# Two transformer blocks on one core: latents' norms in halves, the bias store and the recurrence's weights moved, decay and bonus a round later, feed-forwards begun by channel blocks

## The chip, the core and the metric

The program runs on one core of a Trainium2 chip. A core has five engines that follow their own instruction streams and meet only at semaphores: TensorE (PE in the profile) multiplies matrices into PSUM banks, VectorE (DVE) and ScalarE (ACT) do elementwise work and reductions, GpSimd (POOL) does slower elementwise work, and SyncE (SP) issues DMA transfers. ACT and POOL issue DMAs too. The metric is the device time of the whole program in microseconds (us), and the number that is compared is the median over several executions.

## What is computed

x is 1024 tokens by 1024 channels, everything is float32, and two layers run one after the other. The reference, cut:

```python
# first block
mod = silu(c) @ ada_w + ada_b                 # 1024 -> 6144: six vectors
h = rms_norm(x, mix_pre_norm) * (1 + sc_m) + sh_m
att_p, rwkv_p = split(h @ w_in)               # 456 and 1824 columns
# attention: latents cq (256), ckv (128), index key (64), each with an rms norm
score = sum_h iw[h] * relu(iq[h] @ ik.T)      # causal; the top 256 keys of each query are kept
logits = qa @ ckv_sel + rel_bias[bucket(t - s)]
# recurrence (RWKV7, 8 heads of 64), on p + mu * (p_prev - p)
S = S * w_t + (S @ a_t) b_t + v_t k_t ;  y_t = S @ r_t
y = (groupnorm(y) + sum(r * k * r_k) * v) * g # the sum is the "bonus"
x = x + g_m * rms_norm(concat(att, y) @ w_out)
f = (silu(hf @ w_gate) * (hf @ w_up)) @ w_down    # hf = modulated rms_norm(x), 2816 hidden
x = x + g_f * rms_norm(f)
# second block: short convolution, attention by chunks, gated mix, then
up = causal_conv3(rms_norm(h) @ w_ffn_up) + b     # 2 x 2816
h = h + rms_norm((gelu(f_gate) * f_val) @ w_down) # and a gated per-layer embedding
```

## The kernel before

The kernel is written by hand in one order per engine. Each operation that another waits for raises a counter (`V.up(name)`, `S.up(name)`, `T.up(name)`), and `wait_ge(*X.at(name))` waits for it. An engine never goes past its waiting instruction. `B.free(b)` and `B.until(b, ...)` guard the eight PSUM banks.

**Projection and rows, 0 to 440 us.** x is normalized and transposed to hT. Weights come in pieces of up to 1 MB into five slots. `ROW_LOADS` is the order in which SP issues these loads (`ring_load`, L419), `SLOT_OF` says which slot a piece takes, and SP waits there until the piece that held the slot has been used. PE computes the attention columns (L523), then eight tiles of the first 256 recurrence columns (`("rkv", 0, t)`), then three small matmuls (L579) that turn the relative bias into a row for each head. ACT copies this row (L1021) and issues one DMA (L1023) that stores it 128 times into `bias_rows`, 4.6 MB in all, on its own queue. Attention reads `bias_rows` much later. Then come `LAT_STEPS`: transposes of the normed latents ("turn") and the index queries ("iq"), with one of the `ROW_STEPS` behind every second. Then the index scores with lora columns among them, then the lora columns 1 and 2, then the rest of `ROW_STEPS`. These 56 steps are 40 `("rkv", c, t)`, 256 columns of one token tile, and 16 `("mod", j, q)`, pieces of the modulation whose weights (`in_ada_w`) fill a slot each. An `rkv` step is a group of matmuls on L523, a `mod` step one on L483, with its sum (L502 or L508) behind it.

**The top 256 of each row** are found on DVE by `best_rows`, a generator. Each `next(K.best)` is a pass: count passes (L854, L858) of a bisection, with half of the counting on ACT (`K.sums`, L872), and at the end 24 rank passes (L925 to L937). 223 are needed. The numbers of passes are written out: 30 beside the loras, `passes_beside(i)` beside each row step i, `best_steps(g)` in each round of the recurrence.

**Recurrence, 440 to 866 us.** Eight token tiles go through rounds; tile t starts 7 rounds after tile t - 1. `front_*` (j = 0 to 6) makes the tile's rows, `free_*` the 64 x 64 products (L1266, L1352), `state_*` the state. The fronts of tile 0 lie beside the last row steps (`round_beside`), from i = 43 on. In `front_vector`, j = 4 ends with Pe (L1609), Pm (L1610), krow (L1613) and the bonus sum (L1615). `front_pool` at j = 0 mixes the keys (L1666, L1668), and at VALUES (6, for tile 0: 8) the values (L1673 to L1677).

**The feed-forwards** start at 1150 us (first block) and at 2753 us (second). The normed tokens of a tile (`("normed", ...)`) are transposed by PE (L2319), scaled by DVE (L2333) and ACT (L2347) into `turned`, split into a high and a low part (L2103 on ACT, L2110 on DVE) for a block k of 128 channels and half the tokens, and multiplied by three weight blocks (L2071, L2073, L2075).

Of the kernel before, what the change touches and what calls it, by code (L numbers as in the profile page):

```python
# [19 lines left out]
FILL = -3.0e38  # L20
# [188 lines left out]
def layout(nc, I, out):  # L209
# [52 lines left out]
    scr = region(W1 - 3440, W1)  # L262
# [15 lines left out]
    r = region(HI0, W1 - 3440)  # L278
# [11 lines left out]
    K.top = region(W1 - 48, W1).take("top", 8, 6)  # L290
    K.lprev, K.ikk = K.rl[0], K.rl[1].rearrange("p (t n) -> p t n", t=8)
# [147 lines left out]
def proj_sync(sp, K):  # L439
# [87 lines left out]
def proj_tensor(pe, K):  # L527
# [39 lines left out]
    w, landed = ring_tile(K, ("rkv", 0), 8, 256)  # L567
    pe.wait_ge(*landed.at(("rkv", 0)))
    for t in range(NT):
        b = 2 + (4 + t) % 6  # L570
        pe.wait_ge(*B.free(b))
        token_group(pe, K, b, w, 256, t).then_inc(*T.up(("rkv", 0, t)))
        B.until(b, S, ("rkv", 0, t))
    T.mark(("free", ("rkv", 0)))
    pe.wait_ge(*D["hot"].at("hot"))
    for i, o in enumerate(range(0, 1152, 512)):
        n = min(512, 1152 - o)
        pe.wait_ge(*B.free(2 + i))
        mm = pe.matmul(bank(K, 2 + i)[0:8, 0:n], K.relb[0:33, :], K.oh[0:33, o:o + n], start=True, stop=True, skip_group_check=True)  # L579
        B.until(2 + i, S, ("bias", i))  # L580
    mm.then_inc(*T.up("bias"))
    pe.wait_ge(*V.at("latents"))
    pe.wait_ge(*V.at("modulation 0"))
    for i, step in enumerate(LAT_STEPS):
        lat_tensor(pe, K, step, 2 + 2 * (i % 2))
        if i % 2:
            row_tensor(pe, K, ROW_STEPS[i // 2], ROW_BANK[i // 2])
# [124 lines left out]
def proj_vector(v, K):  # L712
# [51 lines left out]
    v.wait_ge(*S.at(("att", 1, 7)))  # L764
    sq = K.stage[0]
    for j, (a, n, dst) in enumerate(((0, 256, K.att[:, :, 0:256]), (256, 128, K.ckv), (384, 64, K.ikk[:, :, 0:64]))):
        x_ = K.att[:, :, a:a + n]
        v.wait_ge(*V.own())
        v.tensor_tensor(sq[:, :, 0:n], x_, x_, MUL).then_inc(*V.up())
        v.wait_ge(*V.own())  # L770
        v.tensor_reduce(K.st[:, 0:8], sq[:, :, 0:n], AX, ADD).then_inc(*V.up())
        v.wait_ge(*V.own())
        variance(v, K, ("lv", j), K.st[:, 0:8], n, 1e-6)
        v.wait_ge(*G.at(("lr", j)))
        v.tensor_tensor(dst, x_, b8(K.st[:, 16:24], n), MUL).then_inc(*V.up())
    v.wait_ge(*V.own())
    v.wait_ge(*D["m2"].at("m2"))
    v.tensor_tensor(K.ckv, K.ckv, K.kvB.unsqueeze(1).to_broadcast([128, 8, 128]), MUL).then_inc(*V.up())
    v.tensor_tensor(K.ikk[:, :, 0:64], K.ikk[:, :, 0:64], K.ikB.unsqueeze(1).to_broadcast([128, 8, 64]), MUL).then_inc(*V.up())
    v.wait_ge(*V.own())  # L780
    v.tensor_copy(K.ikk[:, :, 64:128], K.ikk[:, :, 0:64]).then_inc(*V.up())
    v.tensor_scalar(K.iw, K.att[:, :, 448:456], float(8 ** -0.5 * 64 ** -0.5), None, MUL).then_inc(*V.up("latents"))
    for i, step in enumerate(LAT_STEPS):
        lat_vector(v, K, step, 2 + 2 * (i % 2))
# [8 lines left out]
    for i in range(ROWS_FIRST, len(ROW_STEPS) + 1):  # L793
        if i == ROWS_FIRST + 4:
# [31 lines left out]
def passes_beside(i):  # L826
    return 4 if ROW_STEPS[i - 1][0] == "rkv" and i <= BESIDE else 2
# [2624 lines left out]
```

## Time and profile before

| | |
|---|---|
| median of 3 runs | 3649.11 us (3641.34 to 3659.92) |
| the profiled execution: its time, its span | 3646.83 us, 3645.5 us |
| PE busy, DVE busy, ACT busy | 3346.4, 1794.3, 928.1 us |
| chain of work that ended last | PE 81%, DVE 11%, ACT 4% |
| TensorE clock, mean over the span | 0.962 of full |

The profile shows one execution. The span is the time from the first to the last instruction. Its stages have different limits, so a stage is read by itself: the windows give busy time and clock of a stretch, the timeline shows behind each row in square brackets how long the engine sat idle before it and what ended that.

### The profile page before, as it was taken

How to read it: one execution, taken by the hardware profiler on the slowest of the kernel's cores; microseconds unless marked ns; L12 is line 12 of the kernel's file. 1: busy time of each engine (PE TensorE's matmuls, PEld its weight loads, DVE VectorE, ACT ScalarE, POOL GpSimd, SP SyncE). 2: the span in 40 equal slices, each digit the busy share in tenths (PEclk: the TensorE clock that was granted, in tenths of full speed). 3: DMA queues.
4: the chain of work that ended last, by engine and by line, in shares of the span. 5: the costliest groups of instructions: out<-in, count | busy, mean ns of one | idle time of the engine just before them, and what ended most of it. 6: DMA issues, size and time to landing. Idle time of an engine off the chain costs nothing.

```text
span 3645.5 us, 51038 instructions
## 1 busy us (share of the span) xinstructions
PE 3346.4 (92%) x21635; PEld 2602.0 (71%) x21650; DVE 1794.3 (49%) x2850; ACT 928.1 (25%) x1709; POOL 339.0 (9%) x278
## 2 busy tenths in 40 slices
PE   7988867887888999999999889999998999999998
PEld 6736655775567788888886556876676888878876
DVE  2378677664556322224545546321246444444656
ACT  2255432333534100001222544000025111111122
POOL 0000245762001000000000000000000000000000
PEclk9989977999999999999999999999999999999999
DMA  6337210101114111113331001111133111123434
GB/s 216 70 65 239 84 42 19 37 20 59 47 64 133 52 47 52 47 47 104 121 118 50 4 24 40 42 35 35 58 116 110 47 47 52 47 75 98 140 115 144
DMA packets 217381, 270.18 MB, mean 74 GB/s; under 512 B 11229, under 2 KB 176387, under 8 KB 216900
## 3 DMA queue, kind: packets, MB, share of 16 engines
q1 hardware_dynamic: 211851, 247.87, 21.3%
q10 hardware_dynamic: 3192, 11.17, 1.7%
q0 software_dynamic: 2112, 7.87, 0.6%
q8 instruction: 173, 2.83, 0.3%
q14 instruction: 53, 0.43, 0.0%
HBM read 232.80 MB, written 34.08 MB: 73 GB/s over the span
## 4 chain that ended last, share of the span: by engine, by line
PE 81%; DVE 11%; ACT 4%; issue 2%; DMA 1%; POOL 1%; SPq 0%; DVEq 0%; ACTq 0%; POOLq 0%
PE psum L2071 18%; PE psum L2073 18%; PE psum L2075 18%; PE psum L523 5%; PE psum L3089 3%; PE psum L1266 2%; PE psum L2589 2%; PE psum L2910 2%; PE psum L2797 2%; PE psum L651 1%; PE psum L1821 1%; PE psum L2926 1%; DVE Lg L1915 1%; PE psum L1847 1%; DMA slot<-in_ada_w 1%
## 5 line engine op out<-in xcount | busy, mean ns | idle before, releaser
L2071 PE MATMUL psum<-hT_hi,wcut_lo 128*128 128x512 f32 x1856 | 589.4, 395 | 16.7 <-DVE hT_lo L2110 16.7
L2073 PE MATMUL psum<-hT_hi,wcut_hi 128*128 128x512 f32 x1856 | 582.8, 391 | 0.0
L2075 PE MATMUL psum<-hT_lo,wcut_hi 128*128 128x512 f32 x1856 | 582.5, 391 | 0.0
L2071 PEld LDWEIGHTS psum<-hT_hi,wcut_lo 128*128 128x128 f32 x1856 | 350.4, 189 | 97.0 <-DVE hT_lo L2110 17.9
L2053 DVE CAST wcut_hi<-raw 128x1024 fp32r<-128x1024 f32 x256 | 176.9, 691 | 478.6 <-PE psum L2075 454.0
L2075 PEld LDWEIGHTS psum<-hT_lo,wcut_hi 128*128 128x128 f32 x1856 | 350.3, 189 | 73.2
L2073 PEld LDWEIGHTS psum<-hT_hi,wcut_hi 128*128 128x128 f32 x1856 | 350.3, 189 | 72.6
L2071 PE MATMUL psum<-wcut_hi,xcut_lo 128*128 128x512 f32 x1120 | 348.7, 393 | 17.6 <-DVE xcut_lo L2189 13.8
L2073 PE MATMUL psum<-wcut_hi,xcut_hi 128*128 128x512 f32 x1120 | 347.2, 392 | 0.0
L2075 PE MATMUL psum<-wcut_lo,xcut_hi 128*128 128x512 f32 x1120 | 346.9, 391 | 0.0
L1097 POOL TENSOR_TENSOR st<-st,nhalf 128x1 f32<-128x1 f32 (+2 forms) x78 | 61.1, 790 | 2827.2 <-DVE st L709 2827.2
L2055 DVE TENSOR_TENSOR wcut_lo<-raw,wcut_hi 128x1024 fp32r<-128x1024 f32 x256 | 313.8, 1226 | 8.8
L2071 PEld LDWEIGHTS psum<-wcut_hi,xcut_lo 128*128 128x128 f32 x1120 | 211.5, 189 | 63.4 <-DVE xcut_lo L2189 15.7
L2073 PEld LDWEIGHTS psum<-wcut_hi,xcut_hi 128*128 128x128 f32 x1120 | 211.9, 189 | 44.3
L2075 PEld LDWEIGHTS psum<-wcut_lo,xcut_hi 128*128 128x128 f32 x1120 | 211.6, 189 | 44.1
L523 PE MATMUL psum<-slot,hT 128*128 128x256 f32 (+1 forms) x1024 | 230.7, 386 | 3.3 <-DMA slot<-in_w_in 3.3
L523 PEld LDWEIGHTS psum<-slot,hT 128*128 128x128 f32 x1024 | 196.5, 197 | 37.7 <-issue 13.7
L2160 ACT ACTIVATE xcut_hi<-fS 128x512 fp32r<-128x512 f32 x88 | 55.1, 632 | 329.8 <-PE psum L2075 325.8
L2495 ACT ACTIVATE fS<-psum 128x1024 f32<-128x1024 f32 x22 | 22.7, 1030 | 427.9 <-PE psum L2075 427.9
L2486 DVE TENSOR_TENSOR fS<-fS,psum 128x1024 f32<-128x1024 f32 x22 | 26.9, 1221 | 190.9 <-PE psum L2075 190.9
L872 ACT ACTIVATE counted<-counted 128x1024 bf16<-128x1024 bf16 (+2 forms) x99 | 93.0, 941 | 70.0 <-DVE counted L854 69.8
L2521 DVE SCALAR_TENSOR_TENSOR tb<-psum,CF,tb 128x1023 f32<-128x1023 f32 x22 | 28.2, 1283 | 135.4 <-ACT tb L2541 135.4
(428 smaller groups left out, 4354.5 us busy)
## 6 DMA issues: line engine op xcount, KB each, us to landing
raw<-in_w_ffn_down SPq DMA_DIRECT2D x88, 512.0 KB, 3.6
raw<-in_w_ffn_up SPq DMA_DIRECT2D x66, 512.0 KB, 3.8
slot<-in_ada_w SPq DMA_DIRECT2D x24, 1024.0 KB, 11.7
raw<-in_w_in SPq DMA_DIRECT2D x28, 512.0 KB, 5.4
raw<-in_w_ffn_gate SPq DMA_DIRECT2D x22, 512.0 KB, 3.9
slot<-in_w_in SPq DMA_DIRECT2D x8, 1024.0 KB, 6.1
raw<-in_w_out SPq DMA_DIRECT2D x16, 512.0 KB, 3.7
x_one<-xrow SPq DMA_DIRECT2D x16, 512.0 KB, 2.8
```

The lines of the kernel that those rows point to most:

```text
L523: mm = pe.matmul(p[:, 0:n], K.hT[:, k, t * 128:(t + 1) * 128], w[:, k, 0:n], start=k == 0, stop=k == 7, skip_group_check=True)
L872: s.activation(a, a, ACT.Copy, accum_out=K.top[:, 0, t - 2:t - 1]).then_inc(*K.S.up(("counted", n, t)))
L1266: mm = pe.matmul(b0[par][half(c), cols64(q, o)], lhs(c, q, par), rhs(c, q, par), start=start, stop=stop, skip_group_check=True)
L2053: v.tensor_copy(hi, raw).then_inc(*K.V.up())
L2055: v.tensor_tensor(lo, raw, hi.bitcast(F), SUB).then_inc(*K.V.up(("cut", name, n)))
L2071: pe.matmul(outs[i], al, bs[i][0], start=start, stop=False, skip_group_check=True)
L2073: pe.matmul(outs[i], ah, bs[i][0], start=False, stop=False, skip_group_check=True)
L2075: mm = pe.matmul(outs[i], ah, bs[i][1], start=False, stop=stop, skip_group_check=True)
L2589: mm = pe.matmul(bank(K, t)[:, 0:n], K.hT2[:, k, t * 128:(t + 1) * 128], w[:, k, :], start=k == 0, stop=k == 7, skip_group_check=True)
L2797: mm = pe.matmul(bank(K, b)[:, 0:n], xT[:, k, t * 128:(t + 1) * 128], w[:, k, :], start=k == 0, stop=k == kt - 1, skip_group_check=True)
L2910: mm = pe.matmul(bank(K, b, 2)[:, o:o + n], K.qT[0:96, h, t * 128:(t + 1) * 128], K.kT2[0:96, h, o:o + n], start=True, stop=True, skip_gro ...
L3089: mm = pe.matmul(bank(K, b, 2)[:, h], K.wo[q % 2][j][:, k, :], xT[:, k, h], start=k == 0, stop=k == 3, skip_group_check=True)
```

## The change

Four things are changed.

1. The latents' norms are done in two halves of four tiles (`norms_vector`), beside the copies of the attention columns. The eight `("rkv", 0, t)` steps now lie among `LAT_STEPS`, and no row step does; all 56 row steps come behind the loras. The bias matmuls, their copies and the store of `bias_rows` lie between the loras and the first row step.
2. `rwkv_weights`, eleven loads on SP's queue that wait for ("shift", 2) on DVE, are issued behind the load of `("mod", 3, 2)`, ahead of that of `("mod", 3, 3)`. The store of the latents is moved ahead of them, the wait for the bias store behind them. The mod steps are spread over 24 rkv steps.
3. 180 passes instead of 140 beside the row steps, and two in each round of the recurrence instead of three (fourteen rounds) or two: 53 were left for it, now 13. krow and bonus go from front round 4 to 5. POOL mixes a tile's keys behind the values of the tile before, and tile 0's values one round earlier.
4. Both feed-forwards begin by channel blocks: PE transposes block k of four tiles into one bank, DVE scales it, ACT and DVE split it, and PE multiplies it by all three weight blocks. Before, weight block 0 came first with all k, then 1, then 2.

Core of the diff:

```diff
-LAT_STEPS = [("turn", t) for t in range(NT)] + [("iq", q) for q in range(4)]
+LAT_STEPS = [("rkv", 0, t) for t in range(5)] + [("turn", 0), ("turn", 1), ("rkv", 0, 5), ("turn", 2), ("turn", 3), ("rkv", 0, 6),
+             ("turn", 4), ("turn", 5), ("rkv", 0, 7), ("turn", 6), ("turn", 7)] + [("iq", q) for q in range(4)]
...
-        if (1, 5) <= (_c, _t) < (3, 5):
+        if _c < 4 and (8 * _c - 8 + _t) % 3:
             ROW_STEPS.append(_mods[sum(s[0] == "mod" for s in ROW_STEPS)])
...
-SLOT_OF = {_s: (1, 3, 4)[_i % 3] for _i, _s in enumerate(_mods)}
-SLOT_OF.update({("rkv", _c): 2 * (_c % 2) for _c in range(2, 6)})
+SLOT_OF = {_s: 1 + _i % 3 for _i, _s in enumerate(_mods)}
+SLOT_OF.update({("rkv", _c): 4 * (_c % 2) for _c in range(1, 6)})
...
         ring_load(sp, K, key, *row_weight(K, key))
-        if key == ("rkv", 4):
+        if key == ("rkv", 2):
+            latents_store(sp, K)
+        if key == MODS[10]:
             rwkv_weights(sp, K)
...
+        if 4 <= t < 7:
+            norms_vector(v, K, 0, t - 4)
+    for part in range(3):
+        norms_vector(v, K, 1, part)
...
-    return 4 if ROW_STEPS[i - 1][0] == "rkv" and i <= BESIDE else 2
+    return 4 if i and ROW_STEPS[i - 1][0] == "rkv" and round_beside(i) is None else 2
...
 def best_steps(g):
-    return 3 if g < 14 else 2
+    return 2
...
         V.mark(("rows read", t))
+    if j == 5:
         v.wait_ge(*G.at(("rk", t)))
         v.tensor_tensor(kn, kn, Pi, MUL).then_inc(*V.up(("krow", t)))
         v.wait_ge(*G.at(("rkk", t)))
...
-VALUES, VALUES_FIRST = 6, 8
+VALUES, VALUES_FIRST = 6, 7
...
-    if j == 0:
+    if t == 0 and j == 0:
         g.wait_ge(*D["mu"].at("mu"))
-        g.wait_ge(*D["raw"].at(t))
-        g.tensor_tensor(prev, prev, mx, SUB).then_inc(*G.up())
-        g.wait_ge(*G.own())
-        g.tensor_tensor(prev, prev, K.muB, MUL).then_inc(*G.up(("mixed", t)))
+        keys_pool(g, K, 0)
...
+    if t and j == VALUES and t + 1 < NT:
+        keys_pool(g, K, t + 1)
...
 def ffn_start_tensor(pe, K, name, P):
+    for n in range(3):
+        pe.wait_ge(*K.V.at(("cut", name, n)))
+    for h in range(2):
+        ahead = len(TURN_BANKS[h])
+        for k in range(ahead):
+            turn_block(pe, K, P, h, k, TURN_BANKS[h][k])
+        for n in range(3):
+            pe.wait_ge(*K.bank.free(2 * n + h))
+        for k in range(8):
+            pe.wait_ge(*K.V.at(("split", name, h, k)))
+            for n in range(3):
+                wh, wl = weight_pair(K, name, n)
+                mm = product3(pe, [bank(K, 2 * n + h)], (wh[:, k, :], wl[:, k, :]), [(K.hi[:, k, tokens(h)], K.lo[:, k, tokens(h)])],
+                              k == 0, k == 7)
+                if h and k == 7:
+                    mm.then_inc(*K.T.up(("used", name, n)))
+            if k + ahead < 8:
+                turn_block(pe, K, P, h, k + ahead, TURN_BANKS[h][k % ahead])
```

**SP, the slot loads and the recurrence's weights.** Before, `wlo` to `muB` (`rwkv_weights`) stood behind eight `in_ada_w` loads and one of `in_w_in` and behind the latents' store:

```order
L419 DMA slot<-in_ada_w 128x8x256 x8
L419 DMA slot<-in_w_in 128x8x256
L1169 DMA latents<-spill 128x4096
L1171 DMA wlo<-in_w_decay_up 64x512
L1172 DMA wlo<-in_w_aaa_up 64x512
L1173 DMA wg<-in_w_gate_up 128x512
L1174 DMA wg<-in_w_gate_up 32x512
L1175 DMA mk<-in_c_table 128x710
L1178 DMA rowB<-in_w 128x512
L1178 DMA rowB<-in_a 128x512
L1178 DMA rowB<-in_k_k 128x512
L1178 DMA rowB<-in_k_a 128x512
```

Now, with the line numbers of the changed kernel, the same loads stand behind the first three `in_ada_w` loads, and the row that follows these is again `in_ada_w`, four of them, the first being `("mod", 3, 3)`:

```order
L426 DMA slot<-in_ada_w 128x8x256 x3
L1202 DMA wlo<-in_w_decay_up 64x512
L1203 DMA wlo<-in_w_aaa_up 64x512
L1204 DMA wg<-in_w_gate_up 128x512
L1205 DMA wg<-in_w_gate_up 32x512
L1206 DMA mk<-in_c_table 128x710
L1208 DMA rowB<-in_w 128x512
L1208 DMA rowB<-in_a 128x512
L1208 DMA rowB<-in_k_k 128x512
L1208 DMA rowB<-in_k_a 128x512
L1208 DMA rowB<-in_r_k 128x512
L1209 DMA muB<-in_mu_shift 128x1024
```

What moved: the eleven loads (`muB` the last) are five `in_ada_w` loads earlier on SP's queue.

**ACT, the copies of the bias row and its store.** Before, they stood behind the copies (`stage`) of the eight `("rkv", 0, t)` tiles, ahead of the turns (`spill`, `ikT`):

```order
L1016 ACTIVATE stage<-psum 128x256 x8
L1021 ACTIVATE oh<-psum 8x512 x2
L1021 ACTIVATE oh<-psum 8x128
L1023 DMA bias_rows<-oh 1024x1x1152
L1067 ACTIVATE spill<-psum 128x128
L1068 ACTIVATE ikT<-psum 128x128
```

Now they stand behind the last lora copy and its tanh, ahead of the copy of the first row step (`stage`):

```order
L1074 ACTIVATE lora<-psum 32x1024
L1080 ACTIVATE lora<-lora 32x1024
L1056 ACTIVATE oh<-psum 8x512 x2
L1056 ACTIVATE oh<-psum 8x128
L1058 DMA bias_rows<-oh 1024x1x1152
L1116 ACTIVATE stage<-psum 128x256
L894 ACTIVATE counted,top<-counted 128x1024
```

What moved: the DMA of `bias_rows` is behind all turns, index queries, scores and loras.

**DVE, front rounds 4 and 5 of tile 1.** Before, krow (`krow<-krow,Pi`) and the bonus (`bon`) followed Pm at once:

```order
L1609 SCALAR_TENSOR_TENSOR Pe<-kk,Pe 128x512
L1610 TENSOR_TENSOR Pm<-Pm,mx 128x512
L1613 TENSOR_TENSOR krow<-krow,Pi 128x512
L1615 TENSOR_REDUCE bon<-tmp 128x8
L854 TENSOR_SCALAR counted<-scores,top 128x896
L854 TENSOR_SCALAR counted<-scores,top 128x768
L858 TENSOR_SCALAR over,top<-scores,top 128x640
```

Now three or four passes and one `TX` of the products stand between them:

```order
L1641 SCALAR_TENSOR_TENSOR Pe<-kk,Pe 128x512
L1642 TENSOR_TENSOR Pm<-Pm,mx 128x512
L959 SCALAR_TENSOR_TENSOR maskb<-over,tied 128x896
L947 TENSOR_SCALAR scores<-scores,top 128x1024
L949 TENSOR_SCALAR over,top<-scores,top 128x1024
L950 TENSOR_SCALAR tied<-scores,top 128x1024
L1383 TENSOR_TENSOR TX<-psum,mk 128x512
L1646 TENSOR_TENSOR krow<-krow,Pi 128x512
L1648 TENSOR_REDUCE bon<-tmp 128x8
```

What moved: krow and bon stand behind the `TX` copy that PE's next product waits for. The passes beside them are already rank passes (`maskb`, `rank`), where before they were count passes.

## Rows read from the trace of the kernel before

**Rows 1.** The page: the chain that ended last, shares by engine
```profile
PE 81%; DVE 11%; ACT 4%; issue 2%; DMA 1%; POOL 1%; SPq 0%; DVEq 0%; ACTq 0%; POOLq 0%
```

**Rows 2.** Timeline of PE, bias matmuls to LAT: start us, us, idle before
```profile
126.57 2.10 PE L579 MATMUL psum<-oh,relb 33*8 33x512 f32 x6
129.91 0.30 PE L667 MATMUL psum<-ident,att 128*128 128x128 f32 x1 [1.24 <-ACT oh L1021]
```

**Rows 3.** Timeline of PE, where the scores begin
```profile
169.68 1.56 PE L651 MATMUL psum<-ikT,iqT 64*128 64x512 f32 x6
```

**Rows 4.** Timeline of DVE, last operation of the latents' norms
```profile
120.32 0.19 DVE L782 TENSOR_SCALAR iw<-att 128x64 f32<-128x64 f32 x1
```

**Rows 5.** Timeline of PE where the row steps go on after the loras
```profile
273.00 1.02 PE L508 MATMUL psum<-sel,mrow 128*128 128x1 f32 x4 [5.41 <-ACT mrow L494]
```

**Rows 6.** Windows of the bias store and the rows stage's end: length, busy, PEclk, DMA share, GB/s
```profile
134.00:229.00 95.00, 88.33 (x329) 44.93 (x328) 45.66 (x56) 39.47 (x65) 1.46 (x5) 0.95 0.50 62
372.00:440.00 68.00, 62.68 (x280) 52.80 (x279) 43.34 (x93) 28.72 (x62) 14.97 (x10) 0.95 0.31 105
```

**Rows 7.** DMA, 202 to 206 us: packets, MB, share of 16 engines
```profile
q10 hardware_dynamic: 42, 0.19, 46.4%
q1 hardware_dynamic: 43, 0.04, 3.1%
```

**Rows 8.** Tile slot, 160 to 175 us: its load and its landing
```profile
L419 SPq DMA_DIRECT2D slot<-in_ada_w x1: 367/367/367, 166.3 to 166.3; - x1
...
DMA to landing us min/median/max: 62.3/62.3/62.3
```

**Rows 9.** Timeline of SP: the first weight load, the next slot loads
```profile
321.98 0.55 SPq L1171 DMA_DIRECT2D wlo<-in_w_decay_up  x1
...
333.72 10.44 SPq L419 DMA_DIRECT2D slot<-in_ada_w  x3
```

**Rows 10.** Timeline of PE, 330 to 375 us: the stall and the steps behind
```profile
347.21 1.93 PE L483 MATMUL psum<-slot,csz 128*32 128x256 f32 x16 [10.62 <-DMA slot<-in_ada_w]
...
354.96 1.07 PE L483 MATMUL psum<-slot,csz 128*32 128x256 f32 x16
...
360.05 1.07 PE L483 MATMUL psum<-slot,csz 128*32 128x256 f32 x16
```

**Rows 11.** Timeline of PE, start of the recurrence
```profile
459.15 1.97 PE L1266 MATMUL psum<-vrow,MK 64*64 64x64 f32 x32 [10.95 <-POOL vrow L1677]
```

**Rows 12.** Timeline of POOL, 440 to 462 us
```profile
450.00 2.34 POOL L1666 TENSOR_TENSOR prev<-prev,mx 128x1024 f32<-128x1024 f32 x1
...
457.41 1.59 POOL L1677 TENSOR_TENSOR vrow<-vrow,prevV 128x512 f32<-128x512 f32 x1
```

**Rows 13.** Windows between starts of Pe (L1609) of tiles 0 to 5
```profile
420.15:478.71 58.56, 31.19 (x372) 25.61 (x370) 38.94 (x65) 20.42 (x43) 23.03 (x17) 0.77 0.19 64
478.71:525.55 46.84, 32.22 (x677) 28.19 (x679) 36.31 (x55) 20.42 (x37) 25.82 (x18) 0.76 0.10 36
525.55:579.76 54.21, 37.61 (x912) 33.58 (x911) 46.58 (x58) 14.31 (x22) 27.14 (x18) 0.85 0.10 31
579.76:648.29 68.53, 48.53 (x985) 40.50 (x982) 51.27 (x52) 16.33 (x26) 36.44 (x23) 0.71 0.08 25
648.29:692.63 44.34, 37.88 (x934) 31.79 (x934) 30.54 (x35) 15.73 (x25) 32.83 (x23) 0.92 0.11 38
```

**Rows 14.** Groups of DVE, 450 to 640 us, its costliest
```profile
L931 DVE TENSOR_TENSOR_SCAN rank<-tied,top 128x384 f32<-128x384 bf16 (+5 forms) x6 | 13.8, 2304 | 0.2
```

**Rows 15.** Timeline of PE, start of the first feed-forward
```profile
1161.43 0.76 PE L2071 MATMUL psum<-hT_hi,wcut_lo 128*128 128x512 f32 x1 [6.08 <-DVE hT_lo L2110]
...
1195.62 0.77 PE L2071 MATMUL psum<-hT_hi,wcut_lo 128*128 128x512 f32 x1 [3.20 <-DVE hT_lo L2110]
```

**Rows 16.** Groups of the first feed-forward's start: the low half of a split
```profile
L2110 DVE TENSOR_TENSOR hT_lo<-hTa,hT_hi 128x512 fp32r<-128x512 f32 x16 | 9.8, 686 | 2.6 <-ACT hT_hi L2103 2.6
```

**Rows 17.** Timeline of PE, start of the second feed-forward
```profile
2795.33 0.77 PE L2071 MATMUL psum<-hT_hi,wcut_lo 128*128 128x512 f32 x1 [2.84 <-DVE hT_lo L2110]
```

More of the change, by code:

```diff
@@ L566, in proj_tensor @@
     T.mark(("free", "att b"))
[L567 to L587, printed above, removed]
+    for step, b in zip(LAT_STEPS, LAT_BANK):
+        lat_tensor(pe, K, step, b)
     for n, (t, q) in enumerate(SCORES):
@@ L594, in proj_tensor @@
             lora_tensor(pe, K, m, n)
-    for i in range(ROWS_FIRST, len(ROW_STEPS) + 1):
+    pe.wait_ge(*D["hot"].at("hot"))
+    for i, o in enumerate(range(0, 1152, 512)):
+        n = min(512, 1152 - o)
+        pe.wait_ge(*B.free(2 * i))
+        mm = pe.matmul(bank(K, 2 * i)[0:8, 0:n], K.relb[0:33, :], K.oh[0:33, o:o + n], start=True, stop=True, skip_group_check=True)
+        B.until(2 * i, S, ("bias", i))
+    mm.then_inc(*T.up("bias"))
+    for i in range(len(ROW_STEPS) + 1):
         if i < len(ROW_STEPS):
             row_tensor(pe, K, ROW_STEPS[i], ROW_BANK[i])
-        if ROW_STEPS[i - 1][0] == "mod":
+        if i and ROW_STEPS[i - 1][0] == "mod":
             mod_sum(pe, K, ROW_STEPS[i - 1], ROW_BANK[i - 1])
@@ L661, in lat_tensor @@
     T, V, S, B = K.T, K.V, K.S, K.bank
+    if step[0] == "rkv":
+        return row_tensor(pe, K, step, b)
     p = bank(K, b, 2)
@@ L762, in proj_vector @@
         v.tensor_copy(K.att[:, t, 0:256], bank(K, 2 + 2 * t % 6)[:, 0:256]).then_inc(*V.up(("att", 0, t)))
[L764 to L784, printed above, removed]
+        if 4 <= t < 7:
+            norms_vector(v, K, 0, t - 4)
+    for part in range(3):
+        norms_vector(v, K, 1, part)
+    V.mark("latents")
+    for step, b in zip(LAT_STEPS, LAT_BANK):
+        lat_vector(v, K, step, b)
     for t, q in SCORES:
@@ L799, in proj_vector @@
         for _ in range(passes_beside(i)):
-            next(K.best)
-        if ROW_STEPS[i - 1][0] == "mod":
+            next(K.best, None)
+        if i and ROW_STEPS[i - 1][0] == "mod":
             mod_vector(v, K, ROW_STEPS[i - 1], ROW_BANK[i - 1])
@@ L942, in lat_vector @@
     T, V, S = K.T, K.V, K.S
+    if step[0] == "rkv":
+        return
     p = bank(K, b, 2)
@@ L1039, in proj_scalar @@
             next(K.sums, None)
[L1040 removed]
+    s.wait_ge(*T.at("bias"))
+    for i, o in enumerate(range(0, 1152, 512)):
+        n = min(512, 1152 - o)
+        s.activation(K.oh[0:8, o:o + n], bank(K, 2 * i)[0:8, 0:n], ACT.Copy).then_inc(*S.up(("bias", i)))
+    s.wait_ge(*S.own())
+    s.dma_start(K.vbd.ap(), K.oh[0:8, :].unsqueeze(1).to_broadcast([8, 128, 1152])).then_inc(*D["bias"].up("bias", 16))
+    for i in range(len(ROW_STEPS) + 1):
+        j = round_beside(i)
         if i < len(ROW_STEPS):
             row_scalar(s, K, ROW_STEPS[i], ROW_BANK[i])
+        if j is not None and j >= 5:
+            front_scalar(s, K, 0, j)
         for _ in range(passes_beside(i)):
             next(K.sums, None)
[L1045 to L1046 removed]
+        if j is not None and j < 5:
+            front_scalar(s, K, 0, j)
 def lora_scalar(s, K, m):
@@ L1062, in lat_scalar @@
     T, V, S = K.T, K.V, K.S
+    if step[0] == "rkv":
+        return row_scalar(s, K, step, b)
     p = bank(K, b, 2)
@@ L2449, in ffn_start_vector, with high_scalar @@
+def high_scalar(s, K, P, h, k):
+    s.wait_ge(*K.V.at(("scaled block", P.name, h, k)))
+    s.activation(K.hi[:, k, tokens(h)], P.turned[:, k, tokens(h)], ACT.Copy).then_inc(*K.S.up(("split", P.after, h, k)))
 def ffn_start_vector(v, K, name, P):
     cut_to(v, K, name, 2)
-    for t in range(4):
-        post_out_vector(v, K, P, t)
-    v.wait_ge(*K.S.at(("turned out", name, 0)))
-    split_vector(v, K, name, P.turned, (0,))
-    tail_vector(v, K, P)
-    v.wait_ge(*K.S.at(("turned out", name, 1)))
```

172 lines of the change are left out of this document (120 added, 52 removed).

## The prediction

> **What bounds the kernel now.** I read the chain that ended last first, then PE's waits, then the stages one by one. PE is 81% of the chain [rows 1], so a term of the sum is time that PE gains or loses, and most of the span (attention, both feed-forwards behind their starts) is not touched. The stages that are: rows, up to 440 us, where PE waits seldom and long [rows 5, 10]; the recurrence, where a tile should take the 44.3 us of the undisturbed interval between two Pe, and takes 46.8, 54.2 and 68.5 as long as DVE also has passes to do [rows 13]; and the two feed-forward starts [rows 15, 17].
>
> **Part 1, latents and bias, ahead of the scores.** The norms end at 120.5 [rows 4], before PE is through with its earlier work at 126.6 [rows 2]; in halves they end some 10 us earlier, and PE's point of need moves from 129.9 to about 116. Both are off the path, so the halves bring nothing by themselves. The scores now begin at 169.7 [rows 3]. Ahead of them six row steps (6 x 3.5 us) and the bias matmuls (2.1 us) go away: start near 146.8, 23 us earlier. None of this is saved, it comes again behind the loras. There PE waits for ACT, which is as far behind as now (5.4 us at 273.0 [rows 5]), and now twice: the bias matmuls for the last lora copy, the first row step for the bias copies. I put 9 us in place of 5.4. The first row step then starts at 250.7.
>
> **Part 2, the bias store meets the slot loads.** This is the largest term. The store is issued at 130 now, right behind the copies for which PE waits until 129.9 [rows 2], and goes on until 229, some 95 us, at half a DMA share [rows 6]: 42 packets of 0.19 MB, so 4.5 KB each, take 46.4% of 16 engines in 4 us [rows 7], which is 0.7 us for one, and the steady half says that it lies on half of the engines. One slot load falls into it: issued at 166.3, it lands 62.3 us later, at the store's end [rows 8]. A look at four microseconds shows why: 43 packets of the load's queue pass for 42 of the store's [rows 7], one for one, although the store's take fifteen times as long each. So 512 packets of 1 KB (the half of a 1 MB load that lies on the shared engines) need at least 48 us. Now only one load meets the store, and PE needs it 100 us after its issue, so it costs nothing.
>
> After the change the store is issued at about 252 and moves from 255 to 350. The loads of the first three mod pieces are in their slots by then. Behind them on SP stand the eleven weight loads, which wait for DVE's third shift (behind the last lora, so with everything there 23 us earlier, about 249) and take 11.7 us to issue (321.98 to 333.72 [rows 9]), so the load of ("mod", 3, 3) is issued at about 260, into the store. Ahead of it in the same queue is half or more of the weights. By its own packets it would land at 255 + 48 = 303, by the measured 62.3 us at 317 to 322, and with the weights' packets ahead at 335 or later; the store's end, 350, is the latest. I take 345. PE reaches this step (i = 9) at 250.7 + 6 x 3.5 + 3 x 1.5 plus 2 for a slow clock, 278, and stalls 67 us; bounds 25 (303) and 72 (350).
>
> What hides it? Nothing: steps 10 and on are queued behind it on PE, and no other work of PE is in reach. DVE and ACT can run their passes ahead, as far as step 20, where DVE waits for a mod step. From step 9 to 40 there are 13 mod and 18 rkv steps. A pair takes 5.09 us (354.96 to 360.05), the pair behind the stall at 347.2, after which the clock was below full, 7.75 [rows 10], that is 2.7 more. 13 x 5.09 + 5 x 3.5 + 2.7 = 86. Step 40 starts at 345 + 86 = 431 instead of 372.1: **+59**.
>
> The Trainium skill ("DMA: Bandwidth & Descriptors", "Queues, rings and completion order") says that an engine alternates between its queue rows by packets, and drains about 9 to 17 descriptors of one row before it switches. If a 1 KB record of the load were one such descriptor, and the store's 4.6 KB one a packet, ten of the load's would pass for each of the store's, and the stall would be gone, a time near 3570. The rows show 43 for 42 instead, and the trace decides; it stays as the first rival.
>
> **Steps 40 to the end of the rows** take 68.0 us with PE 62.7 and DVE 43.3 busy [rows 6]. There are 16 passes more beside them (52 for 36), of which 11 are rank passes, and these are longer: the scan alone is 2.3 us [rows 14]. That is 11 x 1.9 + 41 x 0.8 = 54 us of passes where 28 were, so DVE rises to about 69 of 68. It was given a lead by the stall. I leave 68.0; bounds 65 (ACT's fronts from round 5 on now go ahead of its passes) and 76. Rows end at 499, +59.
>
> **Part 3, the recurrence.** PE's first product waits 10.95 us for POOL's vrow [rows 11]. POOL does tile 1's key mix (2 x 2.3) ahead of tile 0's values [rows 12]. Values now come one round earlier and ahead of the state-free work: -10.5. The rest of this first interval (58.6 us) I count at nothing, though it has two passes a round instead of three, but for 1.5 us that POOL's key mix beside round 5 and the longer rank passes may cost: +1.5. From round 14 on no pass is left, in the middle of the next interval. The intervals 46.8, 54.2 and 68.5 hold PE 32.2, 37.6 and 48.5 busy, at clocks 0.76, 0.85 and 0.71, and the undisturbed one 37.9 at 0.92 in 44.34 [rows 13]. It has the most work in flight; the two before it have less, since the state products of tile 0 begin only in the second of them, and at a clock of 0.92 their 32.2 and 37.6 of PE would be 27 and 35. With the 6.5 us of waits that the undisturbed interval has, 33 to 42; I put 38 for both, and 44.3 for the third: -9, -16 and -24. The rank passes that lay there (six scans are 13.8 us [rows 14], and they are one of six kinds) are done beside the rows. krow and the bonus at j = 5 now stand behind the TX copy for which PE waits, and PE's turn of krow is later; from tile 4 on I count 0, bounds -1.5 and +1.5 a tile. Sum -10.5 + 1.5 - 9 - 16 - 24 = **-58**, bounds -35 (half of each interval's gain) and -68.
>
> **Part 4, feed-forwards.** The first product starts at 1161.4 after 6.1 us of waiting [rows 15], because DVE and ACT scale all eight blocks of tile 3 before the first split. The transposes ended at 1155.3 (1161.4 less 6.1). By blocks only one of tile 3's eight transposes stands before the first split, so it can begin some 0.5 us earlier, and one scaling and the two halves of a split of 512 columns (0.69 for the low one [rows 16]) follow: 1157. The second half starts now at 1195.6, behind four tiles' transposes and a last wait of 3.2; by blocks PE goes on after the last normed tile at about 1182, since the first half's 24 x 3 products fill the time until then, as now. It then carries its own transposes (3.5 us) and a late release of the weight blocks (all three at the very end, where the first was free earlier): -10 at the end of the two halves. In the second feed-forward the same steps save 8, as its second half too begins with such a wait (2.84 [rows 17]), but the next cut stands behind a convolution that waits for the late products, some 4.5 us: -3.5. Together **-13**, bounds -18 and 0.
>
> **Sum.** +59 - 58 - 13 = -12 on the profiled execution's 3646.8: 3634.8. That execution lies 2.3 below the median of the runs, so 3637.
>
> **Rivals.** (a) *The store doesn't hold the loads up* (by the engine's turns, or because the weights and the load pass before the store gets going): 303 at the latest, and in the extreme no stall. For it: only one load shows the effect, and its issue lay 33 us behind the store's start. Against it: 62.3 us [rows 8]. Landing at 303 takes 42 us off the stall, no stall 67: 3570 to 3595. Chance 0.14. (b) *Slower: the rounds without passes don't get short.* If the intervals of tiles 1 to 4 are long by PE's own slow clock (0.71 to 0.85 [rows 13]) and the products' round trips between PE, DVE and ACT, and passes only filled the gaps, taking them away gives half: -30 instead of -58, time 3665. The change is slower by more than it can be told from a gain under 28 us on. For it: DVE is busy 51 of 68.5 us, so it isn't full. Against it: 44.3 as soon as the passes are gone, with the same work. Chance 0.16. (c) *The feed-forwards gain nothing*, since DVE has the same operations to do beside the tail of norms: 3649, within my own range; 0.1. (d) *DVE bounds the end of the rows*: +8 and more, 3644; counted in the range. The likeliest case, all four parts as worked out, has 0.6, with a range of its own from 3618 to 3656.
>
> **How the numbers follow.** About 0.5%, 18 us, is what a measurement of this kernel tells from no change: the three runs lie 18.6 apart. Below 3631 lie (a) and somewhat under half of the likeliest case; above 3667 half of (b) and a bit of the likeliest. So faster 0.42, same 0.45, slower 0.13. The range runs from 3597, which leaves out the extreme of (a), to 3670.
>
> **What would show it.** In the profile after: one wait of PE of 60 to 70 us for a slot load of `in_ada_w`, begun near 278; the load's time to landing over 70 us; rows ending near 499; PE's first product of the recurrence without a wait of 11 us for vrow; Pe to Pe of tiles 1 to 4 near 38, 38 and 44; the first product of the feed-forwards some 4 us nearer to the last of w_out. Wrong would be the prediction above all if the load lands near 300, or if these intervals stay above 50. If both happen they cancel in part, and the total would look right for a wrong reason.

## The result and the profile after

The changed kernel takes 3690.1 us (median of 4 runs, 3683.73 to 3695.3), the kernel before 3645.2 (4 runs). The ratio is 1.0109 with a 95% interval from 1.0081 to 1.0136: slower by 1.1%, where 3637 was forecast with a range up to 3670.

The page of the changed kernel, and PE's longest waits from 99 to 620 us (waited for: us in total, times, longest):

```profile
span 3685.8 us, 50970 instructions
...
PE 3345.5 (91%) x21635; PEld 2595.5 (70%) x21650; DVE 1790.1 (49%) x2834; ACT 911.0 (25%) x1645; POOL 341.9 (9%) x277
...
PE 80%; DVE 9%; POOL 3%; ACT 2%; issue 2%; another core or an unknown queue 2%; DMA 1%; SPq 0%; DVEq 0%; ACTq 0%; POOLq 0%
```

```profile
PE psum L492 <- DMA slot<-in_ada_w: 68.0, 1, 68.0
PE psum L1297 <- DVE TX L1383: 14.5, 5, 6.1
PE psum L1591 <- DVE Pe L1641: 11.5, 3, 5.5
PE psum L1315 <- DVE MK L1374: 7.8, 1, 7.8
...
PE psum L532 <- ACT oh L1056: 4.2, 1, 4.2
```

PE is as busy as before; 40 us more of the span is idle. The one wait of 68.0 us is the forecast stall, at its place and nearly its size. The timeline of PE shows it between the fourth mod step and the one before. The tile view of that slot's load, in a window of 2 us about its issue, shows 77.0 us from issue to landing:

```profile
246.11 9.13 PE L532 MATMUL psum<-slot,hT 128*128 128x256 f32 x32 [4.16 <-ACT oh L1056]
...
273.27 0.50 PE L517 MATMUL psum<-sel,mrow 128*128 128x1 f32 x4
341.75 1.93 PE L492 MATMUL psum<-slot,csz 128*32 128x256 f32 x16 [67.98 <-DMA slot<-in_ada_w]
...
357.17 1.07 PE L492 MATMUL psum<-slot,csz 128*32 128x256 f32 x16
```

```profile
L426 SPq DMA_DIRECT2D slot<-in_ada_w x1: 4295/4295/4295, 264.7 to 264.7; - x1
...
DMA to landing us min/median/max: 77.0/77.0/77.0
```

A window of 4 us within the store, 300 to 304, repeats [rows 7]:

```profile
q10 hardware_dynamic: 43, 0.20, 47.7%
q1 hardware_dynamic: 43, 0.04, 3.1%
```

The recurrence did not give back what was forecast. There is no wait for vrow, but the first product stands behind two others. The timeline of PE at its start, and the timeline of DVE in the same stretch:

```profile
506.94 1.29 PE L1315 MATMUL psum<-rT,bT 64*64 64x64 f32 x26 [7.84 <-DVE MK L1374]
...
513.24 1.97 PE L1297 MATMUL psum<-vrow,MK 64*64 64x64 f32 x32 [1.70 <-DVE RR L1378]
```

```profile
484.77 0.61 DVE L949 TENSOR_SCALAR_CACHE_REDUCE over<-scores,top 128x384 bf16<-128x384 f32 x1
...
486.96 1.02 DVE L953 TENSOR_TENSOR_SCAN rank<-tied,top 128x384 f32<-128x384 bf16 x1
488.01 2.52 DVE L956 SCALAR_TENSOR_TENSOR tied<-rank,tied 128x384 bf16<-128x384 f32 x1
490.56 2.58 DVE L959 SCALAR_TENSOR_TENSOR maskb<-over,tied 128x384 bf16<-128x384 bf16 x1
...
494.89 2.94 DVE L953 TENSOR_TENSOR_SCAN rank<-tied,top 128x512 f32<-128x512 bf16 x1
...
503.13 1.55 DVE L953 TENSOR_TENSOR_SCAN rank<-tied,top 128x640 f32<-128x640 bf16 x1
...
505.73 1.16 DVE L1374 TENSOR_TENSOR MK<-psum,mk 128x1024 f32<-128x1024 f32 x1
```

DVE has rank passes (L947 to L959) from 484.3 on, 34.6 us of them up to Pe of tile 1, so MK (L1374), for which PE waits 7.84 us, comes at 505.7. The windows between the starts of Pe answer to [rows 13] (length, PE, PEld, DVE, ACT, POOL busy, PEclk, DMA share, GB/s):

```profile
476.81:535.54 58.73, 33.17 (x395) 26.72 (x393) 54.19 (x65) 12.44 (x24) 26.62 (x16) 0.75 0.17 57
535.54:577.51 41.97, 28.12 (x670) 24.15 (x670) 34.75 (x31) 12.67 (x19) 27.47 (x18) 0.82 0.12 39
577.51:617.55 40.04, 34.11 (x926) 30.11 (x926) 23.74 (x29) 14.37 (x22) 25.73 (x18) 0.96 0.13 43
617.55:663.00 45.45, 39.16 (x934) 33.22 (x934) 29.79 (x36) 15.86 (x25) 33.00 (x23) 0.89 0.11 37
663.00:710.04 47.04, 39.94 (x934) 33.36 (x934) 29.79 (x35) 15.76 (x25) 32.99 (x23) 0.89 0.11 36
```

And the feed-forwards lost time. The timeline of PE in the first, to be held against [rows 15]:

```profile
1177.54 3.54 PE L2487 MATMUL psum<-ident,yw 128*128 128x128 f32 x20 [3.60 <-DVE wcut_lo L2096]
...
1206.68 0.77 PE L2112 MATMUL psum<-hT_hi,wcut_lo 128*128 128x512 f32 x1 [2.02 <-DVE hT_lo L2528]
...
1213.21 0.80 PE L2112 MATMUL psum<-hT_hi,wcut_lo 128*128 128x512 f32 x1 [1.50 <-DVE hT_lo L2528]
...
1218.83 0.50 PE L2112 MATMUL psum<-hT_hi,wcut_lo 128*128 128x512 f32 x1 [1.50 <-DVE hT_lo L2528]
...
1223.11 0.50 PE L2112 MATMUL psum<-hT_hi,wcut_lo 128*128 128x512 f32 x1 [1.50 <-DVE hT_lo L2528]
...
1241.09 0.74 PE L2112 MATMUL psum<-hT_hi,wcut_lo 128*128 128x512 f32 x2 [0.76 <-DVE wcut_lo L2096]
```

Behind 1206.68, six blocks, 1 to 6, each wait 1.50 us for the low part of its split. The timeline of DVE ahead of one of them (1223.11): the scaling of the next block (L2516) waits for PE, and the low part (L2528) stands behind it.

```profile
1221.65 0.81 DVE L2516 TENSOR_SCALAR hTa<-psum,AB 128x512 f32<-128x512 f32 x1 [2.88 <-PE psum L2487]
1222.38 0.68 DVE L2528 TENSOR_TENSOR hT_lo<-hTa,hT_hi 128x512 fp32r<-128x512 f32 x1
```

Where time went, from starts of the same operation in both traces, in us:

| stretch, from and to | before | after | difference |
|---|---|---|---|
| start to Pe of tile 0 | 420.2 | 476.8 | +56.7 |
| Pe of tile 0 to Pe of tile 7 | 361.2 | 324.6 | -36.6 |
| Pe of tile 7 to w_out's first copy (DVE, yw) | 322.2 | 325.6 | +3.4 |
| that copy to the second block's latents (wlat) | 803.1 | 807.1 | +4.0 |
| wlat to the second block's last yw copy | 846.9 | 848.4 | +1.5 |
| that copy to the end | 892.0 | 903.3 | +11.3 |

The sum is +40.3, the difference of the spans. The +3.4 is no part of the change: attention takes 164.7 us from its first to its last product of queries and keys before, at a granted clock of 0.97, and 168.4 after, at 0.94. In the twelve kernels below it reads 164.6 to 165.6 at 0.96 or 0.97 in seven and 168.1 to 168.6 at 0.94 in the others, whatever was edited.

The other rows hold such differences too. e2_ffn_only below has the code of the kernel before up to the feed-forwards, and reads 414.0 in the first row and 334.1 in the third. Part of its first row is the clock from the first score product to the last lora product: 93.4 us at 0.91 before, 87.5 at 1.00 in e2_ffn_only, 88.0 at 1.00 after. So the +56.7 would be some 5 us more but for a higher clock, which e2_ffn_only had without the change.

### The profile page after: what moved, and what is told of

It reads as the page before. It is cut to its first block, busy times and chain, and to the rows that moved or that the text cites. A ratio compares the mean times of both kernels' runs of the same rounds, so it can differ in the third digit from the quotient of the medians.

```text
span 3685.8 us, 50970 instructions
## 1 busy us (share of the span) xinstructions
PE 3345.5 (91%) x21635; PEld 2595.5 (70%) x21650; DVE 1790.1 (49%) x2834; ACT 911.0 (25%) x1645; POOL 341.9 (9%) x277
## 4 chain that ended last, share of the span: by engine, by line
PE 80%; DVE 9%; POOL 3%; ACT 2%; issue 2%; another core or an unknown queue 2%; DMA 1%; SPq 0%; DVEq 0%; ACTq 0%; POOLq 0%
PE psum L2112 18%; PE psum L2116 18%; PE psum L2114 18%; PE psum L532 5%; PE psum L3191 3%; PE psum L2691 2%; PE psum L1297 2%; PE psum L3012 2%; PE psum L2899 2%; PE psum L1862 1%; PE psum L3028 1%; PE psum L648 1%; DVE Lg L1956 1%; PE psum L1888 1%
## 5 line engine op out<-in xcount | busy, mean ns | idle before, releaser
L1121 POOL TENSOR_TENSOR st<-st,nhalf 128x1 f32<-128x1 f32 (+3 forms) x77 | 62.2, 814 | 2836.8 <-DVE st L710 2836.8
L2112 PEld LDWEIGHTS psum<-wcut_hi,xcut_lo 128*128 128x128 f32 x1120 | 212.2, 190 | 63.2 <-DVE xcut_lo L2230 15.1
```

Source lines behind the costliest of these rows:

```text
L2112: pe.matmul(outs[i], al, bs[i][0], start=start, stop=False, skip_group_check=True)
```

## Experiments

Each was timed beside the kernel before on the same chip (medians of that kernel 3646.3, 3645.2 and 3648.9 in the three groups).

### The bias store and the slot loads

**e1_bias_early.** The three bias matmuls, their copies and the store stand ahead of the latents' steps, on PE and on ACT:

```diff
+    pe.wait_ge(*D["hot"].at("hot"))
+    for i, o in enumerate(range(0, 1152, 512)):
...
+    mm.then_inc(*T.up("bias"))
     for step, b in zip(LAT_STEPS, LAT_BANK):
         lat_tensor(pe, K, step, b)
```

> The changed kernel, with the bias matmuls, their copies and the store of bias_rows moved ahead of the latents' steps (issue near 104 us, so the store is over by 205). Theory: the 68.0 us for which TensorE waits for the load of (mod, 3, 3) come from the store alone, one packet of the store for one of the load's queue. Then the wait is gone and the time is 3690 - 68 - 5 (the two waits for ACT at the bias) = 3617, give or take 6. Rival: the passes on VectorE, which ran ahead during the wait, now bound the rows, so that only 40 us come back: 3650.

3614.4 us (ratio 0.9909, 0.9889 to 0.9929). The store is issued at 104.2; in PE's waits up to 440 us no slot load is left:

```profile
PE psum L1315 <- DVE MK L1374: 8.3, 1, 8.3
PE psum L648 <- ACT rl L1105: 6.7, 11, 1.0
```

One edit of place takes 76 us away. The wait was 68.0 of it, and the two waits for ACT at the bias (5.4 and 4.2) are gone too. In the traces, the time from the last lora product to Pe of tile 0 goes from 242.6 to 163.3 us, 79 less. Up to that lora product this execution is 11 us later than the changed kernel, 7 of them at a lower clock (0.89 for 1.00). The rival, that the passes would bound the rows, is out.

**e4_weights_late.** The eleven weight loads behind ("rkv", 4) again:

```diff
-        if key == MODS[10]:
+        if key == ("rkv", 4):
             rwkv_weights(sp, K)
```

> The changed kernel, with the eleven weight loads of the recurrence back behind the load of (rkv, 4) on SyncE's queue. Theory: the load of (mod, 3, 3), issued near 251 instead of 265, has only its own 512 packets on the engines that it shares with the store and lands near 303, at most 320, instead of 341.7; but the loads behind it, needed one after the other every 5 to 8 us, meet the store too (each 48 us if one alone passes), so that the rows wait for them until the store ends near 345, and only 5 to 15 us are saved: 3675 to 3685. Rival: the weights are the whole cause of the wait: 3630 or less.

3694.8 us (1.0131, 1.0109 to 1.0152), no gain at all. The timeline of PE:

```profile
319.81 1.94 PE L492 MATMUL psum<-slot,csz 128*32 128x256 f32 x16 [47.15 <-DMA slot<-in_ada_w]
...
342.99 1.94 PE L492 MATMUL psum<-slot,csz 128*32 128x256 f32 x16 [11.96 <-DMA slot<-in_ada_w]
```

The load of the fourth mod step is issued at 255.2 and lands at 319.8, 22 us earlier than in the changed kernel; its 64.6 us are near the 62.3 of [rows 8]. PE then waits again, until 343, for a load that was issued at 260.2, and the store's last packet ends at 341. So the weights ahead of a load only decide which load is late; the store's end decides when the rows go on. The expectation had the mechanism and 5 to 15 us too much.

### The feed-forward starts

**e2_ffn_only.** The kernel before with the new `ffn_start_*`, nothing else.

> The kernel before, with only the two feed-forward starts of the change. Theory: in the second half each block's split stands on VectorE behind the scaling of the next block, which waits for a transposition that TensorE does behind the products of the block before, so TensorE waits 1.5 us a block; the profile of the changed kernel then gives + 4 us in the first and + 11 in the second feed-forward: 3645 + 15 = 3660. Rival (my prediction): a saving of 13, 3632. Second rival: the shift in the trace comes from the clock or from what lies ahead: 3645.

3665.2 us (1.0051, 1.0033 to 1.0070), 18.9 slower than before. In its trace the first feed-forward stretch of the table takes 807.1 (+4.0) and the second 907.1 (+15.1), with the same row of waits of 1.50. So this part alone, forecast at -13, costs 19. Its profiled execution is one of the longer ones (3674.5 us), mostly by the third row of the table, ahead of the feed-forwards; the two stretches alone give the same 19.

**e3_lo_first.** The order on DVE in the second half:

```diff
-    if k < 7:
+    if k < 7 and not (h and k):
         scaled_vector(v, K, P, h, k + 1)
...
+    if k < 7 and h and k:
+        scaled_vector(v, K, P, h, k + 1)
```

> The changed kernel, where VectorE makes the low part of block k ahead of the scaling of block k + 1 in the second half of both feed-forward starts (from k = 1 on). Theory of the serial chain: the waits of 1.5 us before each block's products go (7 or 8 in each), and with them some of the slow clock (0.86): 10 to 15 us each, 3690 - 24 = 3666. Rival: TensorE is then held by the scaling of the next block instead, or the clock sets the pace: 3685 to 3690.

3663.3 us (1.0048, 1.0030 to 1.0065), 26.8 less than the changed kernel. In the traces the two feed-forward stretches are 10.7 and 9.9 shorter, and another 3.3 is attention, which is not this edit's. The timeline of PE, where the six waits of 1.50 were:

```profile
1203.45 0.77 PE L2112 MATMUL psum<-hT_hi,wcut_lo 128*128 128x512 f32 x1 [2.02 <-DVE hT_lo L2528]
...
1224.08 0.50 PE L2112 MATMUL psum<-hT_hi,wcut_lo 128*128 128x512 f32 x1 [0.29 <-DVE hT_lo L2528]
...
1227.17 0.73 PE L2112 MATMUL psum<-hT_hi,wcut_lo 128*128 128x512 f32 x2 [0.73 <-DVE wcut_lo L2096]
```

The second half takes 23.7 us (1203.45 to 1227.17) instead of 34.4. The low part of block k needs only its own scaling and its high part; it had been queued behind the scaling of block k + 1, which waits for a transposition that PE reaches only behind the products of block k - 1. So each block paid a round trip PE, DVE, PE.

**e5_early_lo and e6_early_oldffn.** Both mends together, and the early store with the old feed-forward starts.

> The changed kernel with both edits that gave time back: the bias store ahead of the latents' steps, and the low part of block k ahead of the scaling of block k + 1 in the second half of the feed-forward starts. Theory: the two lie in different stages and add: 3614 - 26 = 3588. Rival: something behind takes part of it back: 3600 or more.

> The changed kernel with the bias store ahead of the latents' steps and the feed-forward starts of before. Theory: the new starts cost 15 to 19 us as they were written, so 3614 - 17 = 3597. With e5_early_lo at 3588, channel blocks are worth some 9 us once VectorE's order is mended. Rival: blocks bring nothing even then, and both kernels read the same.

3591.3 (0.9847, 0.9821 to 0.9873) and 3590.9 (0.9844, 0.9818 to 0.9869). The mends add up (3614.4 less 26.8 is 3587.6). In the whole time the mended channel blocks bring nothing that can be measured: the rival of the second expectation holds. By the stretches of the table, in e8_early_lo_one the first feed-forward takes 796.4 (-6.7) and the second 893.4 (+1.4), so some 5 us remain, within the scatter of the medians.

**f1_ffn2_old.** The second feed-forward as before, the first with mended blocks.

> e8_early_lo_one with the second feed-forward's start as before (the first keeps the mended channel blocks). Theory: blocks pay in the first (the second half begins 13 us earlier in the stage), but in the second they are given back, because all three weight blocks are released only at the end and the next cut comes 4.4 us late behind a convolution; so 3 to 6 us faster than e8_early_lo_one. Rival: blocks are worth nothing in either, and both kernels read the same.

3582.4 (0.9827, 0.9802 to 0.9852), 2.3 less than e8_early_lo_one's 3584.7, within the scatter. The stretch of the second feed-forward goes from 893.4 to 890.8. The wait that the prediction named is there in e8_early_lo_one, the next cut behind the convolution:

```profile
2752.28 1.22 PE L2112 MATMUL psum<-hT_hi,wcut_lo 128*128 128x512 f32 x2 [4.41 <-DVE wcut_lo L2096]
```

### The recurrence

**f3_passes_53.** e5_early_lo with 51 passes left for the recurrence:

```diff
-    return 4 if i and ROW_STEPS[i - 1][0] == "rkv" and round_beside(i) is None else 2
+    return 4 if 0 < i <= 22 and ROW_STEPS[i - 1][0] == "rkv" else 2
...
 def best_steps(g):
-    return 2
+    return 3 if g < 14 else 2
```

> e5_early_lo with 51 of the 223 passes left to the recurrence instead of 13 (142 beside the row steps, three a round up to round 13, then two), as before the change. Theory: the whole gain of the recurrence comes from the passes, so the intervals of tiles 1 to 4 go back to some 47, 54 and 68 us from 42, 40 and 45: 3591 + 38 = 3629, less 3 that the rows may win. Rival: part of it came from GpSimd's order and from krow's place, and only 15 to 20 us are lost.

3617.8 us (0.9924, 0.9897 to 0.9950), 26.5 more than e5_early_lo. Its windows between the starts of Pe:

```profile
397.48:443.02 45.54, 29.30 (x371) 24.22 (x369) 37.30 (x64) 20.81 (x41) 23.06 (x16) 0.84 0.26 82
443.02:495.84 52.82, 32.07 (x657) 27.83 (x659) 39.76 (x61) 18.78 (x33) 25.11 (x18) 0.76 0.10 31
495.84:546.68 50.84, 37.43 (x941) 33.01 (x940) 45.60 (x51) 14.25 (x22) 28.39 (x18) 0.90 0.10 33
546.68:612.28 65.60, 47.26 (x976) 39.23 (x972) 50.49 (x49) 16.33 (x26) 37.05 (x23) 0.73 0.08 26
```

The long intervals come back (52.8, 50.8, 65.6), so they were the passes'. But the first is 45.5, against 58.6 before and 58.7 after: with count passes in it instead of rank passes, 13 us come out of it. Four intervals sum to 214.8 here, to 228.1 before, to 186.2 after. Bringing the passes forward is worth 28.6, and the rest of the change (GpSimd's order, krow's place, and two passes fewer, which this run doesn't part) 13.3. The next three intervals sum to 169.3 here and 169.6 before, so all of that rest lies in the first one. Bringing the passes forward then costs 13.2 in the first interval (45.5 to 58.7) and gains 41.8 in the other three.

**e8_early_lo_one.** `best_steps` returns 1, so that the 13 passes spread over twice the rounds.

> e5_early_lo with one pass of the top-256 search in each round of the recurrence instead of two, so that the 13 that are left end at round 19 and not at 13. Theory: the rank passes stand ahead of MK on VectorE (wait of 8 us) and fill 54 of the 58.7 us of the first interval; those ahead of it in the last row steps stay, so half of the first interval's excess goes, and the next interval (VectorE busy 35 of 42) takes some back: 3 to 6 us faster than e5_early_lo. Rival: the passes only move, and the two read the same; or they push the second interval: 5 us slower.

3584.7 (0.9832, 0.9804 to 0.9859), 6.6 less than e5_early_lo; the first interval is 53.6 instead of 58.7 (and 50.6 in f1_ffn2_old, which has the same code there, so some 3 us are scatter). The wait for MK is still 7.8, since the rank passes ahead of it belong to the last row steps.

**f2_pool_before.** GpSimd's order as before, on top of that:

> e8_early_lo_one with GpSimd's part of the recurrence as before: each tile's keys mixed in its own round 0, tile 0's values in round 8 behind the masks. Theory: TensorE's first product again waits 11 us for vrow, since VectorE no longer is the later one there, so the first interval is 3 to 8 us longer: 5 us slower than e8_early_lo_one. Rival: VectorE's passes still hide it and both read the same. Were the prediction's minus 10.5 right here, it would be 10 us slower.

3581.6 (0.9822, 0.9794 to 0.9850), not told from e8_early_lo_one by the scatter. The wait for vrow is back, and the wait for MK has shrunk from 7.83 to 1.52:

```profile
425.61 0.80 PE L1313 MATMUL psum<-rT,bT 64*64 64x64 f32 x26 [1.52 <-DVE MK L1372]
...
439.23 1.98 PE L1295 MATMUL psum<-vrow,MK 64*64 64x64 f32 x32 [9.62 <-POOL vrow L1715]
```

The two waits are 11.1 us together, against 7.8, so the passes don't hide GpSimd here, as the rival had it. The first interval is 54.9, against 53.6 and 50.6 with the new order: 1 to 4 us, and not 10.5. The expectation of 5 us on the whole time was wrong for another reason: the four intervals from Pe of tile 3 to Pe of tile 7 sum to 177.6, against 185.1 in e8_early_lo_one. What the old order loses at the start it gains later, and the total doesn't show either.

**e7_early_lo_krow4.** krow and the bonus in front round 4 again:

> e5_early_lo with krow and the bonus sum back in front round 4. Theory: a tile's interval is set by the waits for Pe and by TensorE's work, so it is 0 to 1.5 us a tile longer or shorter at most, the time within 8 us of e5_early_lo. Rival: krow in round 4 stands ahead of TX, for which TensorE waits, with GpSimd slowing it (1.67 us instead of 0.69): 2 us a tile, 12 to 15 us slower.

3587.3 (0.9839, 0.9813 to 0.9866), 4 less than e5_early_lo, not told from it by the scatter. The windows of two late tiles, in e5_early_lo and in e7_early_lo_krow4:

```profile
545.38:590.87 45.49, 39.33 (x934) 33.40 (x934) 29.78 (x35) 15.86 (x25) 33.02 (x23) 0.89 0.11 37
590.87:637.95 47.08, 39.95 (x934) 33.41 (x934) 29.78 (x36) 15.74 (x25) 33.02 (x23) 0.89 0.11 36
```

```profile
594.43:638.77 44.34, 37.84 (x934) 31.74 (x934) 30.35 (x35) 15.74 (x25) 32.80 (x23) 0.92 0.12 38
638.77:683.91 45.14, 38.12 (x934) 31.89 (x934) 30.78 (x35) 15.74 (x25) 32.79 (x23) 0.92 0.11 38
```

With krow in round 5 a tile takes 45.5 or 47.1 us at a clock of 0.89 here, with round 4 44.3 or 45.1 at 0.92; from Pe of tile 3 to Pe of tile 7 that is 185.1 against 178.2. But the move is not enough by itself: f2_pool_before has krow in round 5 too, with GpSimd's old order, and takes 177.6. And e1_bias_early, with the recurrence of the changed kernel, has two intervals of 44.0 and 44.1 among longer ones (181.6 in all). So the longer intervals, 1 to 3 us a tile in most tiles, come where both edits meet, and taking back either one gives some 7 us of them back in the trace (4.0 and 3.1 in the medians, within their scatter). Why is not shown.

**f4_best.** What single edits had given, together: one pass a round, krow in round 4, the first feed-forward mended with the waits for the cuts behind the first transpositions, the second as before.

> The combination that the runs point to: bias store ahead of the latents' steps, one pass a round, krow and the bonus in front round 4, mended channel blocks in the first feed-forward with the waits for the weight cuts behind the first transpositions, the second feed-forward's start as before. Adding what single edits gave: 3585 - 4 (second feed-forward) - 4 (krow) - 2 (waits for the cuts) = 3575. Rival: the small terms don't add and it reads 3582 or more.

3578.2 (0.9818, 0.9790 to 0.9846): 70.7 us less than the kernel before beside it, and 112 less than the changed kernel. Between it, f1_ffn2_old and f2_pool_before nothing can be told apart. The waits for the cuts behind the first transpositions give next to nothing: the first feed-forward's stretch is 795.8, against 796.4 in e8_early_lo_one.

## Why the prediction was wrong

**Latents and scores: right.** The norms in halves end at 110.4, PE needs them at 116.0 and doesn't wait, and the scores begin near 146, all as forecast. No run takes the halves back by themselves.

**The bias store and the loads (+59): right.** The wait is 68.0 us against 67, begins near 274, and ends at 341.8 against 345. Pe of tile 0 comes 56.7 later. The store's issue was at 246.2, 6 us ahead of the forecast, and the wait's end came 3 us ahead. Most of that lead is the clock of 1.00 up to the last lora product, which the forecast didn't count on, so the closeness of 56.7 to 59 is good to some 5 us only. e1_bias_early gives the wait back whole.

**Feed-forwards (-13): wrong, and the larger error.** The failed step is the second half, "It then carries its own transposes (3.5 us) and a late release of the weight blocks". Its start was right: with the stage's start 23.5 us later, the measured 1206.7 is 1183.2 against 1182. Its length was taken as PE's own work, some 20 us (72 products at 0.23 us, and 3.5), and is 34.4, because the working didn't ask what is queued ahead of the low part on DVE; in e3_lo_first, with that order mended, it is 23.7. In e2_ffn_only the whole part measures +19, an error of 32 us. A smaller thing was missed too: PE's first transpositions now wait 3.60 us for the third weight cut, for which only the products need to wait. f4_best shows that it cost little: without it PE waits 0.89 and 2.37 us there for ACT's yw.

**The recurrence (-58): right in mechanism for the later intervals, wrong for the first.** Measured in the trace: -36.6. Of the 21 us that are missing, 9 lie in the first interval, 7 in the next three, and 5 in tiles 5 and 7. The steps -9, -16 and -24 came out as -4.9, -14.2 and -23.1 (intervals 42.0, 40.0 and 45.5). The step that failed is "Values now come one round earlier and ahead of the state-free work: -10.5", with the rest of the interval "at nothing". The wait for vrow went, and a wait for MK of 7.8, one for RR of 1.7 and longer ones for TX took its place, because the passes ahead of round 14 are now rank passes: DVE is busy for 54.2 of 58.7 us, 34.6 of them with these. The interval stayed at 58.7, where 49.6 was forecast. The 69 of 68 us that I had worked out for DVE at the end of the rows pointed at this; I booked it as a bound of the rows and not as a delay of what stands behind. Where DVE has only count passes there (f3_passes_53), the interval is 13 us shorter, more than the 10.5. Tiles 5 and 7 took 2.7 us more each, beyond the bound of 1.5 a tile. Taking back krow's place (e7_early_lo_krow4) or GpSimd's order (f2_pool_before) gives most of that back in the traces.

**Rivals.** (a) did not come; the one window with 43 packets for 42 was enough. (b), half of the recurrence's gain, came in size (-37 for -58) but not in kind, since the passes did set the intervals. (c), no gain from the feed-forwards, was on the right side and too mild: none of my cases had this part as a loss, and with this part at +15 in the trace (+19 by e2_ffn_only), and -37 in place of -58, the sum 57 - 37 + 15 + 5 is the 40 that the trace shows.

## What to carry to other kernels

When a producer is split into blocks, write down for each block what its engine has queued ahead of it, and what those wait for: an operation that looks ahead (the scaling of block k + 1) must stand behind the one that the consumer waits for now. When one of two inputs of a wait is made earlier, look at what the other one will then cost, above all when work has just been moved onto its engine. And a long store in large packets on another queue delayed the loads here by packets, not by bytes, until it ended; it belongs where no load is waited for. Last, compare a stretch with another execution of the same code before giving its difference to an edit: here such pairs lie 3 to 12 us apart.

## What the runs showed of the hardware

The store (1024 packets of 4.6 KB, 4.7 MB) and the slot loads share engines one packet for one, and a deeper queue of loads doesn't change it (43 and 43 packets in 4 us, with a load landing after 77.0 us). The Trainium skill ("DMA: Bandwidth & Descriptors", "Queues, rings and completion order") has each engine take turns between its queues by packets, which agrees; that a turn drains 9 to 17 descriptors doesn't, if a record of 1 KB is one descriptor. A late interval of the recurrence takes from 43.2 us at a clock of 0.96 over 44.3 at 0.92 to 47.1 at 0.89 or 0.85, with the same 934 matmuls, and short and long ones lie side by side in one execution. And attention reads 164.7 us at a clock of 0.97 or 168.4 at 0.94 from one profiled execution to the next, with the same code; what sets the clock there is not shown.
